# The gate of the expert branch, moved from the copy out of PSUM to the sum of each token's two experts

## The reference, cut to what matters

```
h = modulate(rmsnorm(x, norm2_g[l]), sh2, sc2)
x = x + g2 * moe(h)              # g2: one row of 1024 gate values for all tokens
moe: every token goes to 2 of 16 experts, with weights w0, w1
     yb = (silu(xb @ w_gate[e]) * (xb @ w_up[e])) @ w_down[e]
     moe(h)[token] = w0 * yb(expert 0) + w1 * yb(expert 1)
```

## Time and profile before

| | |
|---|---|
| profiled execution, its own time | 1715.8 us |
| its span | 1714.2 us |
| median of three runs | 1715.42 us |
| TensorE busy | 1474.9 us, 86% of the span |
| VectorE busy | 1227.3 us, 72% |
| ScalarE busy | 750.1 us, 44% |
| mean granted TensorE clock | 0.954 of full speed |

### The profile page before, as it was taken

One profiled execution on the slowest core, in us unless ns is written; L12 is line 12 of the kernel. 1 busy time (PEld: TensorE's weight loads), 2 busy tenths in 40 slices (PEclk: granted clock), 3 DMA queues, 4 the chain that ended last, 5 costly groups with the idle time before them and its releaser, 6 DMA issues.

```text
span 1714.2 us, 18619 instructions
## 1 busy us (share of the span) xinstructions
PE 1474.9 (86%) x6648; PEld 1165.6 (68%) x6648; DVE 1227.3 (72%) x1689; ACT 750.1 (44%) x1037; POOL 138.4 (8%) x185
## 2 busy tenths in 40 slices
PE   1499999999984999999839999999998499999990
PEld 0377877678873777777637787767887377777770
DVE  5476466655465999999866646665546599999993
ACT  1222333232222777777722243322223277777761
POOL 1100000000001111110020000000000111111002
PEclk9999999999996999999969999999999699999995
DMA  8555326454337699999975532645333769999974
GB/s 330 221 172 197 111 99 222 160 185 147 111 125 243 250 389 388 382 385 371 337 276 172 197 111 99 221 151 194 136 109 121 249 244 388 391 383 385 368 256 171
DMA packets 108559, 404.87 MB, mean 236 GB/s; under 512 B 13616, under 2 KB 13616, under 8 KB 107696
## 3 DMA queue, kind: packets, MB, share of 16 engines
q1 hardware_dynamic: 89664, 327.19, 52.7%
q0 software_dynamic: 18800, 76.46, 12.2%
HBM read 376.28 MB, written 34.66 MB: 240 GB/s over the span
## 4 chain that ended last, share of the span: by engine, by line
PE 70%; DVE 15%; issue 4%; DMA 3%; ACT 3%; DVEq 2%; POOL 1%; POOLq 0%; ACTq 0%
PE ps L1196 22%; PE ps L1198 21%; PE ps L1197 20%; DVE w_lo L1053 7%; ACT w_hi L566 2%; PE ps L1264 2%; PE ps L1319 1%; DVE ada_acc L687 1%; PE ps L1294 1%; DMA ada_add<-ada_rows 1%; DMA y_pair<-y_rows,slot_i 1%; PE ps L1298 1%; DMA xg<-h_rows,idx 1%; ACT w_hi L453 1%; PE ps L1354 1%
## 5 line engine op out<-in xcount | busy, mean ns | idle before, releaser
L1053 DVE TENSOR_TENSOR w_lo<-raw,w_hi 128x1024 fp32r<-128x1024 f32 x360 | 424.4, 1220 | 21.6 <-ACT w_hi L566 17.9
L566 ACT ACTIVATE w_hi<-raw 128x1024 fp32r<-128x1024 f32 x360 | 367.5, 1055 | 45.5 <-PE ps L1198 45.5
L453 ACT ACTIVATE w_hi<-raw 128x1024 fp32r<-128x1024 f32 x136 | 142.6, 1058 | 446.2 <-PE ps L1198 423.3
L1196 PE MATMUL ps<-w_hi,hT_lo 128*128 128x512 f32 x832 | 329.2, 396 | 7.3 <-DVE tmp L768 7.2
L1197 PE MATMUL ps<-w_lo,hT_hi 128*128 128x512 f32 x832 | 325.4, 391 | 0.0
L1198 PE MATMUL ps<-w_hi,hT_hi 128*128 128x512 f32 x832 | 325.3, 391 | 0.0
L673 DVE TENSOR_TENSOR w_lo<-raw,w_hi 128x1024 fp32r<-128x1024 f32 x136 | 162.1, 1222 | 163.5 <-ACT w_hi L453 158.5
L1196 PE MATMUL ps<-w_hi,xgT_lo 128*128 128x512 f32 x512 | 208.0, 406 | 4.4 <-DVE xgT_lo L1042 1.3
L1198 PE MATMUL ps<-w_hi,xgT_hi 128*128 128x512 f32 x512 | 202.2, 395 | 0.0
L1197 PE MATMUL ps<-w_lo,xgT_hi 128*128 128x512 f32 x512 | 201.6, 394 | 0.0
L1196 PEld LDWEIGHTS ps<-w_hi,hT_lo 128*128 128x128 f32 x832 | 157.1, 189 | 57.7 <-issue 21.5
(11 more groups left out here) (225 smaller groups left out, 1779.4 us busy)
## 6 DMA issues: line engine op xcount, KB each, us to landing
raw<-w SPq DMA_DIRECT2D x608, 512.0 KB, 5.3
y_rows<-y_out POOLq DMA_DIRECT2D x32, 512.0 KB, 5.3
ahead<-w SPq DMA_DIRECT2D x4, 2048.0 KB, 12.4
x_state<-x POOLq DMA_DIRECT2D x2, 2048.0 KB, 10.8
x<-x_state POOLq DMA_DIRECT2D x2, 2048.0 KB, 9.3
h_rows<-h_nat POOLq DMA_DIRECT2D x8, 512.0 KB, 2.9
y_rows<-x_state POOLq DMA_DIRECT2D x2, 1536.0 KB, 13.1
shift_row<-mod_rows POOLq DMA_DIRECT2D x5, 512.0 KB, 6.5
```

The lines of the kernel that those rows point to most:

```text
L453: act.activation(w_hi[:, q % W_SLOTS], raw[:, r % RAW_SLOTS], ACT.Copy).then_inc(w_hi_ready, 1)
L566: act.activation(w_hi[:, n % W_SLOTS], expert_piece(e, n), ACT.Copy).then_inc(w_hi_ready, 1)
L1053: v.tensor_tensor(w_lo[:, n % W_SLOTS], expert_piece(e, n), w_hi[:, n % W_SLOTS], ALU.subtract).then_inc(raw_used, 1)
L1196: pe.matmul(dst, a_lo, b_hi, start=start, stop=False)
```

## The change

ScalarE takes over the copy of the two PSUM banks, as a plain copy at the end of its own expert body. VectorE no longer does it. The gate is multiplied in after the gather, once for each token tile; ScalarE scales the second expert's rows by their weights first. ScalarE's order at the end of the layer becomes: scale tile t, then the deviations of tile t-1. The overflow branch, not taken here, changes in the same way.

```diff
         def _(act):                                  # ScalarE
+            act.sem_inc(y_copied, 1)                 # (was in VectorE's block)
...
+                act.wait_ge(w_used, q0 + (MIX + EXP + W_SLOTS))        # end of expert(l, e)
+                act.wait_ge(row_stored[odd], l * 160 + (e // 2) * 16 + 32)
+                for half in range(2):
+                    one = act.activation(y_out[:, odd, 512 * half:512 * half + 512], ps[:, 2 + half], ACT.Copy)
+                one.then_inc(y_copied, 1)
+
+            def scale_second(l, t):
+                act.wait_ge(pair_in[t], l * 32 + 32)
+                act.activation(y_pair[:, t, 1], y_pair[:, t, 1], ACT.Copy, scale=wts[:, 4 + t:5 + t]).then_inc(pair_scaled, 1)
...
+            for t in range(NT):
+                act.wait_ge(x_final, t + 1)
+                row_deviations(t)
             for l in range(DEPTH):
-                for t in range(NT):
-                    act.wait_ge(x_final, l * NT + (t + 1))
-                    row_deviations(t)
...
-            for t in range(NT):
-                act.wait_ge(x_final, DEPTH * NT + (t + 1))
-                row_deviations(t)
+                for t in range(NT):                  # at the end of layer l
+                    scale_second(l, t)
+                    if t:
+                        act.wait_ge(x_final, (l + 1) * NT + t)
+                        row_deviations(t - 1)
+                act.wait_ge(x_final, (l + 1) * NT + NT)
+                row_deviations(NT - 1)
...
         def _(v):                                    # VectorE
-                v.wait_ge(w_used, q0 + (MIX + EXP + W_SLOTS))
-
-                v.wait_ge(row_stored[odd], l * 160 + (e // 2) * 16 + 32)
-                for half in range(2):
-                    cols = slice(512 * half, 512 * half + 512)
-                    one = v.tensor_tensor(y_out[:, odd, cols], ps[:, 2 + half], gate_row[:, cols], ALU.mult)
-                one.then_inc(y_copied, 1)
...
                 for t in range(NT):
-                    v.wait_ge(pair_in[t], l * 32 + 32)
-                    v.scalar_tensor_tensor(x[:, t], y_pair[:, t, 0], wts[:, t:t + 1], x[:, t], ALU.mult, ALU.add)
+                    v.wait_ge(pair_scaled, l * NT + (t + 1))
+                    v.scalar_tensor_tensor(y_pair[:, t, 0], y_pair[:, t, 0], wts[:, t:t + 1], y_pair[:, t, 1], ALU.mult, ALU.add)
                     v.drain()
-                    v.scalar_tensor_tensor(x[:, t], y_pair[:, t, 1], wts[:, 4 + t:5 + t], x[:, t], ALU.mult,
-                                           ALU.add).then_inc(x_final, 1)
+                    v.tensor_tensor(y_pair[:, t, 0], y_pair[:, t, 0], gate_row[:], ALU.mult)
+                    v.drain()
+                    v.tensor_tensor(x[:, t], x[:, t], y_pair[:, t, 0], ALU.add).then_inc(x_final, 1)
```

More of the change, by code:

```diff
@@ L364, in build @@
         slots_ready = sem("slots_ready")
+        pair_scaled = sem("pair_scaled")
         pair_in = [sem(f"pair_in{i}") for i in range(NT)]
@@ L656, in _ @@
             v.sem_inc(raw_used, RAW_SLOTS)
-            v.sem_inc(y_copied, 1)
             v.sem_inc(acc_free, 4)
@@ L1162, in _ @@
                         v.wait_ge(ov_step, b * OV_STEPS + 21)
-                        v.tensor_tensor(o_y[:, 0:512], ps[:, 2], gate_row[:, 0:512], ALU.mult)
-                        v.tensor_tensor(o_y[:, 512:1024], ps[:, 3], gate_row[:, 512:1024], ALU.mult).then_inc(ov_step, 1)
+                        v.tensor_copy(o_y[:, 0:512], ps[:, 2])
+                        v.tensor_copy(o_y[:, 512:1024], ps[:, 3]).then_inc(ov_step, 1)
                         v.drain()
```

## The result

The changed kernel takes 1725.87 us (median of four runs, 1725.35 to 1726.46); the kernel before took 1713.78 us over its four runs. The ratio is 1.0072, 95% interval 1.0055 to 1.0090: 12 us slower, where +11.5 had been forecast (1727.3 us). The profiled execution took 1725.35 us with a span of 1723.8, 9.6 us more than the span before.

The account below looks back on a forecast made before the run. It took a loop through TensorE, ScalarE and VectorE, with y_out off it, to set the expert period; uncovered VectorE work bounds layer ends. 0 + 0 + 6.3 + 5.2 = +11.5 us gave 1727.3 us; 8-in-10 range 1720 to 1732.

Parts of the forecast that it names:

- Part 1: Expert stages: y_out leaves VectorE 30 times, 1.19 us each; forecast gain 0, at most 27 us.
- Part 2: Expert stages: ScalarE's two added copies, 1.09 us a pair, 30 times; forecast cost 0, at most 13 us.
- Part 3: Last expert of each layer: gathers start earlier, -0.4 us in all; later weight loads in layer 0, +0.2 us.
- the second term: End of layer 0: weight loads start later, closer to the gathers; +0.2 us, bounds -1 to +1.
- Part 4: Combination at each layer's end: first scaling and three VectorE instructions a tile; with Part 3, +6.3 and +5.2 us.
- A: Expert stage: VectorE's own occupancy is the bound; 27 us gained against 11.5 lost, 1700 us; chance 0.07.
- B: Expert stage: ScalarE's copies delay piece 4 and the loop; 0.42 us a period, 13 us, 1740 us; chance 0.05.
- C: Layer ends: slowly arriving gathers hide the combination's cost; no visible difference, about 1718 us; chance 0.06.
- the loop: Expert stage: xgT_lo, six TensorE pieces, transposes, hidT_hi, piece 8's high half, VectorE's pieces 8 to 13; sets the period.

Follow-up runs that it names:

- e1: Changed kernel with the old two-instruction combination, the expert gate left out: 1713.71 us, ratio 1.0007 to the kernel before.
- e5: Kernel before plus one unused 128x512 multiply on VectorE ahead of y_out in each expert: 1723.11 us, ratio 1.0055.
- e6: Changed kernel plus two unused 128x512 copies on ScalarE ahead of y_out in each expert: 1728.23 us, ratio 1.0079 to the kernel before.
- e12: Changed kernel, ScalarE making three of the next layer's four high halves before copying y_out in layer 0's last expert: 1728.33 us, ratio 1.0089 to the kernel before.
- e2: Changed kernel with y_out copied and gated on VectorE again, new combination kept, so gated twice: 1724.85 us, ratio 1.0074 to the kernel before.
- e10: Changed kernel reordered: xgT_hi, xgT_lo before piece 13, piece 8's high half before hidT_hi, second hidT_lo before VectorE's piece 11: 1708.20 us.
- e11: Kernel before, y_out on VectorE, in the same order as e10: 1714.90 us, ratio 1.0014 to the kernel before.
- e7: Kernel before reordered: xgT_hi, xgT_lo before piece 13, ScalarE's high halves of pieces 8 and 12 before hidT_hi: 1690.99 us, ratio 0.9863.
- e8: Changed kernel in the same order as e7: 1703.09 us, ratio 0.9946 to the kernel before.
- e9: e10 with GpSimd multiplying by the gate, except each layer's last expert on VectorE, and the old combination: 1749.75 us, ratio 1.0215 to the kernel before.

## Why the prediction was right, point by point

- **Part 1, y_out off VectorE, 0 us of a possible 27.** Right. e1 shows it by itself, the unchanged period in both profiles, and e5 gives the size of the slack that was read from two small gaps, 0.25 and 0.05 us: 0.30 us measured. VectorE's new idle time is divided otherwise than forecast, 0.31 us before pieces 4 and 5 and 0.76 before tmp (0.5 and 0.6).
- **Part 2, ScalarE's copies, 0 us of a possible 13.** Right: 1.07 us for the pair where 1.09 was worked out, and the sigmoid's 1.60 us wait unchanged. e6 shows that almost a microsecond more would have fitted in.
- **Part 3, the ends, -0.4 and +0.2.** The sign of the second term was right and its size wrong. The copies are 0.2 us shorter, but the first tile's second gather in layer 0 took 1.2 us longer to land, where I had taken 0.2 and given 1 as the bound. This is the term that was mis-sized. The low halves came only 0.8 us later against TensorE's end, not the 1.5 worked out (855.83 - 852.72 = 3.11 us against 856.27 - 853.99 = 2.28), so it was not the shift that I had too small but what it costs. e12 and the comparison behind it show that the landing goes with the time at which the halves free the slots for the weight loads. In layer 1, where I had no term for it, the same gather landed 0.4 us sooner; it varies by 0.6 us there between kernels.
- **Part 4, +6.3 and +5.2 us with part 3.** Right in layer 0, nearly to the tenth: 3.81 us a tile forecast and measured, the scaling 1.13 to 1.15 (1.15), the late third tile 0.17 (0.19), 16.57 us from the landing to the norm (16.62). With part 3 it is +7.3 measured against +6.3. In layer 1 the +5.1 against +5.2 is in part luck: the combination took 16.92 us where 16.62 had been worked out, mostly for the 0.44 us at which VectorE stood still in the first tile, and the gather that landed 0.4 us sooner made up for it. e2 gives 12.0 us in the medians for this part alone, and 10.9 in the two ends of its profile (11.7 forecast).
- **The sum.** The two ends together cost 12.4 us in the profile, 0.9 more than forecast, nearly all of it the gather of layer 0; with the -0.4 of the expert stages that is 12.0, where the medians have 12.1.
- **The rivals.** A is out in the order of this kernel; e10 and e11 show an order in which y_out on VectorE does cost time in each period. B is out by e6. C is out by e2.
- **The Trainium skill's rule** that the engine with the highest occupancy is the most contended and should be optimized first (Perfetto Trace Analysis, "Identifying the Most-Contended Engine") picked VectorE with 97%. The measurement decides against it here: 1.1 us less of VectorE's work in each 19 us changed nothing, where VectorE was busy 97% of the time (e1) and where it was busy 99% (e7 against e8). The advice of that page to find the gaps on an engine and what blocks it there, which stands in its next section, "Optimization Strategy", and not in the same one as the prediction says, was the one that led to the loop, and with it to e7.

What stays open: the loops read for e7, e8 and e10 are not tested by a run; the 0.44 us in layer 1 has no cause in the trace; and the mixer stages differ by some us from one execution to the next. For these the profiles show what goes with it: from the reciprocal at the end of layer 0 to the first tmp of layer 1 it takes 488.9 to 490.7 us in the nine profiles whose mean granted clock in this stretch is 0.95, and 491.5 to 493.6 in the five with 0.94. Why the clock differs is not shown.

## What to carry to other kernels

An engine that is busy 97% of a stage need not be its bound: if one small wait is left in each period, follow it back through the engines until the loop closes, and ask first whether the work to be moved is on that loop. The slack beside it can be small (0.30 us in e5). Here the move cost 12 us because it put three instructions, and a scaling ahead of the first of them, in place of two where nothing covers them, at the end of each layer, while a new order of the same instructions gained 22 us.

Before moving work off an engine, ask what it costs at the place where it arrives, and count every instruction of a chain with its drain; such a count held to a tenth of a microsecond in layer 0 and to 0.3 in layer 1. What it did not hold was a transfer that meets other transfers: there the term of 0.2 us became 1.2.

## What the runs showed of the hardware that I had not expected

- A multiply of 128x1024 on GpSimd (2.63 us) held VectorE's two-input instructions up by 2.2 us (e9).
- The last store of layer 0, 512 KB, landed after 2.9 us in the kernel before and after 7.3 us beside the earlier weight loads of e12. The landing of the first tile's second gather goes with where the loads of the next layer fall: 5.3 to 7.7 us in layer 0, against 5.2 to 5.8 in layer 1 without them.
- Nearly a microsecond of added ScalarE work a period (e6) left no trace in the period at all.
